# Gate rows, Q squares, row writes and the first one-hot of a two-layer decoder trunk, reordered

## The reference, cut to what matters

```
h = concat(meta, x)                                   # (272, 1024)
# layer 0: mLSTM mixer, 4 heads, q/k width 128, v width 256
q, k, v, o, gates = split(rmsnorm(h) @ w_in)
gates = 15 * tanh((gates + b) / 15);  i, f = gates
b = cumsum(log_sigmoid(f));  the weight of key s for query t in a head:
    exp(b_t - b_s + i_s - m_t)  for s <= t,  m_t = running maximum
out = (sum of s(q,k) * weight * v) / max(|sum|, exp(-m_t)), rmsnorm, * sigmoid(o)
h += out @ w_out
h += moe(rmsnorm(h))
# layer 1: forgetting attention, 16 heads of 64, queries are the 256 real tokens
k, v, f_pre = split(rmsnorm(h) @ kv_w);  F = cumsum(log_sigmoid(f_pre + b_f))
p = softmax(rmsnorm(q) . rmsnorm(k) + F_t - F_s, causal)
h += (p @ v) @ w_o
h += moe(rmsnorm(h))
# moe: 4 groups of 4 experts; best group, the 2 best experts in it;
#      y = sum over both of gate * down(silu(x @ w_gate) * (x @ w_up)), expert width 256
```

## Time and profile before

| | |
|---|---|
| median of 3 runs | 614.47 us (613.95 to 614.58) |
| the profiled execution, in all | 614.16 us |
| its span, first to last instruction | 612.4 us |
| PE busy | 592.6 us, 97% of the span |
| DVE, ACT, POOL busy | 214.0, 146.7, 42.2 us |
| read from HBM | 146.27 MB, 244 GB/s over the span |
| mean granted clock of TensorE | 0.997 |

### The profile page before, as it was taken

One profiled execution on the slowest core, in us unless ns is written; L12 is line 12 of the kernel. 1 busy time (PEld: TensorE's weight loads), 2 busy tenths in 40 slices (PEclk: granted clock), 3 DMA queues, 4 the chain that ended last, 5 costly groups with the idle time before them and its releaser, 6 DMA issues.

```text
span 612.4 us, 8078 instructions
## 1 busy us (share of the span) xinstructions
PE 592.6 (97%) x3098; PEld 369.8 (60%) x3098; DVE 214.0 (35%) x621; ACT 146.7 (24%) x408; POOL 42.2 (7%) x87
## 2 busy tenths in 40 slices
PE   8998999999999999999998999999999899999996
PEld 4686878887764544444466777777777633333331
DVE  3343013331065444444364333333411443222222
ACT  3312123331141111111063333333411421111110
POOL 7010000000011100000003100000000111000000
PEclk9998999999999999999999999999999999999999
DMA  9979430034645999999998614030317599999971
GB/s 284 341 187 347 173 137 1 0 138 155 250 150 220 413 409 424 418 421 380 352 349 252 216 38 170 20 118 1 137 70 274 188 341 355 414 421 420 423 323 70
DMA packets 59123, 150.04 MB, mean 245 GB/s; under 512 B 10092, under 2 KB 42924, under 8 KB 46796
## 3 DMA queue, kind: packets, MB, share of 16 engines
q1 hardware_dynamic: 54384, 136.58, 60.0%
q0 software_dynamic: 2912, 10.64, 5.0%
q10 hardware_dynamic: 1788, 2.29, 1.1%
HBM read 146.27 MB, written 3.23 MB: 244 GB/s over the span
## 4 chain that ended last, share of the span: by engine, by line
PE 91%; DMA 3%; DVE 2%; ACT 2%; issue 1%; SPq 0%; DVEq 0%; ACTq 0%; POOLq 0%
PE bank L1384 38%; PE bank L1656 19%; PE bank L1684 9%; PE bank L1698 5%; PE bank L1628 3%; PE bank L1703 3%; PE bank L1488 1%; DMA qk_area<-xs,idx 1%; PE bank L1825 1%; DMA ring<-in_m_w_in 1%; PE bank L1838 1%; PE bank L1869 1%; PE bank L1865 1%; PE bank L1663 1%; PE bank L1525 1%
## 5 line engine op out<-in xcount | busy, mean ns | idle before, releaser
L1384 PE MATMUL bank<-hxT,ring 128*128 128x272 f32 x576 | 139.5, 397 | 1.2 <-ACT big L647 1.1
L1384 PEld LDWEIGHTS bank<-hxT,ring 128*128 128x128 f32 x576 | 109.0, 192 | 23.8 <-ACT big L647 1.5
L1656 PE MATMUL bank<-ring,gate_area 128*64 128x512 f32 x496 | 115.1, 597 | 0.0
L1656 PEld LDWEIGHTS bank<-ring,gate_area 128*64 128x64 f32 x496 | 34.5, 137 | 63.4 <-issue 62.6
L1384 PE MATMUL bank<-tok,ring 128*128 128x272 f32 (+1 forms) x256 | 59.6, 389 | 0.7 <-DVE tok L1361 0.6
L1684 PE MATMUL bank<-ring,gate_area 128*32 128x512 f32 (+1 forms) x368 | 58.0, 594 | 0.0
L1384 PEld LDWEIGHTS bank<-tok,ring 128*128 128x128 f32 x256 | 47.8, 190 | 11.8 <-issue 3.9
L1096 DVE TENSOR_TENSOR qk_area<-qk_area,bank 128x256 f32<-128x256 f32 x16 | 6.7, 421 | 92.3 <-ACT qk_area L750 92.3
L1684 PEld LDWEIGHTS bank<-ring,gate_area 128*32 128x32 f32 (+1 forms) x368 | 16.5, 119 | 36.3 <-issue 36.3
L533 POOL DMA_INDIRECT qk_area<-xs,idx x16 | 15.8, 985 | 316.4 <-DMA xs<-tok 204.2
L750 ACT ACTIVATE qk_area<-bank 128x256 f32<-128x256 f32 x16 | 6.2, 384 | 121.6 <-PE bank L1656 121.6
(11 more groups left out here) (301 smaller groups left out, 642.8 us busy)
## 6 DMA issues: line engine op xcount, KB each, us to landing
ring<-in_moe_w_gate SPq DMA_DIRECT2D x31, 1024.0 KB, 8.4
ring<-in_moe_w_up SPq DMA_DIRECT2D x31, 1024.0 KB, 11.5
ring<-in_moe_w_down SPq DMA_DIRECT2D x31, 1024.0 KB, 15.0
ring<-in_m_w_in SPq DMA_DIRECT2D x12, 1024.0 KB, 11.6
ring<-in_kv_w SPq DMA_DIRECT2D x8, 1024.0 KB, 12.0
ring<-in_m_w_out SPq DMA_DIRECT2D x4, 1024.0 KB, 13.2
ring<-in_f_w_q SPq DMA_DIRECT2D x4, 1024.0 KB, 12.0
ring<-in_f_w_o SPq DMA_DIRECT2D x4, 1024.0 KB, 7.3
```

Source lines behind the costliest of these rows:

```text
L1384: ins = pe.matmul(bank[c % 2][:, 0:n], w[:, k, half * P:half * P + P], x[:, k, 0:n], start=(k == 0), stop=(k == KB - 1))
L1656: ins = pe.matmul(bank[1][s, :], xgT[b % 2][:, q, s], unit_gate_up(us[par][0], q), start=(q == 0), stop=(q == KB - 1))
```

## The change

It has these parts:

- PE spreads the gate rows of heads 0 and 1 ahead of V's block 0 and those of heads 2 and 3 ahead of block 1. The odd heads' m rows go to bank 4 instead of bank 2, so head 1 waits for DVE's copy of `c_tok` (new semaphore `c_read`). The wait for the last read of an m row moves from V to the first scores.
- In layer 1's first turn ACT squares Q before it handles the forget gates.
- ACT no longer issues the writes of the rows. It signals `rows_made` after each tile and goes on; SP issues the writes, behind the loads of the first two pairs.
- PE folds the logits after half of the first tile's transposes.
- LIVE is added to the base of the places. The one-hot matrix of the first pair is made from the places of its two experts and `eall`, ahead of limits and choices, and only in the first choice's part of `sel`; its indices sum three products (layer 0) instead of six.
- The evacuation of the first half of the first pair's transposed rows is split in two.
- The three units beside the ring share one semaphore.

```diff
         def arrived(s):
             if s in BESIDE:
-                return sem(f"beside_arrived{BESIDE.index(s)}"), 16
+                return sem("beside_arrived"), 16 * len(BESIDE)
...
                 for b in (0, 1):
                     down(b)
+                tiles, n, off = tiles_of(l)
+                for t, rows, c0 in tiles:
+                    sp.wait_ge(*in_layer("rows_made", l, t + 1))
+                    r0 = (META, META + P, 0)[t] - off
+                    sp.dma_start(xs[l][r0:r0 + rows, :], tok[0:rows, t, :]).then_inc(sem("xs_written"), 16)
...
-                act.activation(emB[:, hd, :], bank[(7, 2)[hd % 2]][:, 0:NT], ACT.Exp, scale=2.0) \
+                act.activation(emB[:, hd, :], bank[(7, 4)[hd % 2]][:, 0:NT], ACT.Exp, scale=2.0) \
...
-                    link(ins)
-                    r0 = (META, META + P, 0)[t] - off
-                    act.dma_start(xs[l][r0:r0 + rows, :], tok[0:rows, t, :]).then_inc(sem("xs_written"), 16)
+                    ins.then_inc(sem("rows_made"), 1)
...
+                act.wait_ge(*in_layer("rows_made", l, len(tiles)))
                 act.sem_inc(sem("xr_read"), 1)
...
                     head_rstd(0, "kT", j, NT)
+                    head_square(1, "qT", j, SEQ)
                     if j == 0:
                         act.wait_ge(sem("gate_rows_dve"), 3)
                         link(act.activation(f_a, f_a, ACT.Exp, scale=-1.0))
                         act.activation(f_a, f_a, ACT.Ln, bias=1.0).then_inc(sem("gate_rows_act"), 1)
-                    head_square(1, "qT", j, SEQ)
...
-            link(ins)
+            ins.then_inc(sem("c_read"), 1)
+            dve.wait_ge(sem("c_read"), 1)
...
+                share = [P, nt, 2, CAP]
+                first = sel[:, 0, 0:nt, 0:P].rearrange("p t (e s) -> p t e s", e=2)
+                link(dve.tensor_tensor(first, iota_f[:, 0:P].rearrange("p (e s) -> p e s", e=2).unsqueeze(1).to_broadcast(share),
+                                       raw[:, :, 0:2].unsqueeze(3).to_broadcast(share), ALU.is_equal))
+                dve.tensor_tensor(first, first, eall[:, 0:nt, 0:2].unsqueeze(3).to_broadcast(share), ALU.mult) \
+                    .then_inc(sem("sel_ready"), 1)
                 lim = lim16[:, :].unsqueeze(1).to_broadcast(bc16) if l == 0 else lim16t[:, :, :]
                 link(dve.tensor_tensor(mk[:, 0:nt, :], raw, lim, ALU.is_lt))
-                link(dve.scalar_tensor_tensor(slots[:, 0:nt, :], mk[:, 0:nt, :], LIVE, raw, ALU.mult, ALU.add))
+                link(dve.tensor_tensor(slots[:, 0:nt, :], mk[:, 0:nt, :], raw, ALU.mult))
...
+                row_of_slot(l, 0, 0, 1, 1)
                 link(dve.tensor_reduce(tok4[:, 0:2, 0:nt], t16[:, :, 0:nt, :], AX.X, ALU.add))
-                ones = [P, 2, nt, P]
-                dve.tensor_tensor(sel[:, :, 0:nt, 0:P], iota_f[:, 0:P].unsqueeze(1).unsqueeze(1).to_broadcast(ones),
-                                  tok4[:, 0:2, 0:nt].unsqueeze(3).to_broadcast(ones), ALU.is_equal) \
-                    .then_inc(sem("sel_ready"), 1)
...
-                row_of_slot(l, 0, 0, 1, 1)
...
+                    w = 2 if b == 0 else 4
+                    for q in range(0, 4, w):
+                        dve.tensor_tensor(xgT[b % 2][:, q:q + w, :], bank[0][:, q * P:(q + w) * P].rearrange("p (q s) -> p q s", q=w),
+                                          gains_x[:, l, q:q + w].unsqueeze(2).to_broadcast([P, w, P]), ALU.mult) \
+                            .then_inc(sem("xT_read0"), 1)
...
-            for hd in range(MH):
+            def spread_gates(hd):
+                if hd == 1:
+                    pe.wait_ge(sem("c_read"), 1)
                 if hd >= 2:
                     pe.wait_ge(sem("warg"), hd - 1)
                     pe.wait_ge(sem("em_ready"), hd - 1)
...
-            pe.wait_ge(sem("em_ready"), MH)
             pe.wait_ge(sem("hT_in"), KB)
             for j in range(9):
+                if j < 2:
+                    spread_gates(2 * j)
+                    spread_gates(2 * j + 1)
                 if j < 8:
                     project("v0", j, xT, NT)
...
                     pe.wait_ge(sem("warg"), MH)
+                    pe.wait_ge(sem("em_ready"), MH)
...
-                stream_rows(*tiles[0])
+                stream_rows(*tiles[0], k1=KB // 2)
                 pe.wait_ge(*in_layer("lgT_ready", l, 1))
...
                 ins.then_inc(sem("lg_tr"), 1)
+                stream_rows(*tiles[0], k0=KB // 2)
...
-                    terms = [(c, t, rows) for c in (0, 1) for t, rows, _ in tiles]
+                    terms = [(c, t, rows) for c in ((0,) if part == 1 else (0, 1)) for t, rows, _ in tiles]
...
                         if b == 0 and q == 2:
+                            pe.wait_ge(*in_layer("xT_read0", l, 2))
                             rows_of_slots(3, 3, (2, 3))
```

More of the change, by code:

```diff
@@ L1075, in x_evac @@
                         dve.wait_ge(*in_layer("gu_done", l, b - 1))
-                    dve.tensor_tensor(xgT[b % 2][:, 0:4, :], bank[0][:, :].rearrange("p (q s) -> p q s", q=4),
-                                      gains_x[:, l, 0:4].unsqueeze(2).to_broadcast([P, 4, P]), ALU.mult) \
-                        .then_inc(sem("xT_read0"), 1)
+                    w = 2 if b == 0 else 4
[3 more added lines that the diff above has]
+                            .then_inc(sem("xT_read0"), 1)
                 def combine_weights(b):
@@ L1454, in _ @@
                     .then_inc(sem("negM_mm"), 1)
-                pe.matmul(bank[(7, 2)[hd % 2]][:, 0:NT], negsel2[:, hd, :], row_m, start=True, stop=True) \
+                pe.matmul(bank[(7, 4)[hd % 2]][:, 0:NT], negsel2[:, hd, :], row_m, start=True, stop=True) \
                     .then_inc(sem("em_mm"), 1)
-            pe.wait_ge(sem("em_ready"), MH)
             pe.wait_ge(sem("hT_in"), KB)
             for j in range(9):
+                if j < 2:
+                    spread_gates(2 * j)
+                    spread_gates(2 * j + 1)
                 if j < 8:
@@ L1534, in moe, with stream_rows @@
                 per = 8 if l == 0 else 4
-                def stream_rows(t, rows, c0):
-                    for k in range(KB):
+                def stream_rows(t, rows, c0, k0=0, k1=KB):
+                    for k in range(k0, k1):
                         ins = pe.transpose(bank[(4, 6, 0)[t] + k // 4][0:rows, (k % 4) * P:(k % 4 + 1) * P],
@@ L1623, in rows_to_cols @@
                         if b >= 1:
-                            pe.wait_ge(*in_layer("xT_read0", l, b + 1))
+                            pe.wait_ge(*in_layer("xT_read0", l, b + 2))
                         else:
@@ L1631, in gate_up @@
                 def gate_up(b):
-                    pe.wait_ge(*in_layer("xT_read0", l, b + 1))
+                    pe.wait_ge(*in_layer("xT_read0", l, b + 2 if b else 1))
                     if b >= 1:
```

12 lines of the change are left out of this document (6 added, 6 removed).

## The result

The changed kernel takes 609.4 us (median of 5 runs, 608.07 to 610.52), against 614.58 (613.95 to 620.45, 5 runs) of the kernel before on the same chip: a ratio of 0.9891, 95% interval 0.9855 to 0.9927. The profiled execution took 609.40 us with a span of 607.5, 4.76 less than the 614.16 of before. The forecast was 607.9 with a range of 606.5 to 610.2: the direction and the largest terms were right, the sum 1.5 us too large. The result lies in the wide range, but outside the 607.1 to 608.9 that the forecast itself was given, and next to the 609.6 of rivals A and B; A did not happen, and B did only in one of the two layers.

The account below looks back on a forecast made before the run. PE, 91% of the chain, was taken to bound the kernel, which ends earlier only where PE idles, runs at half clock or does less. Gains 2.7 + 1.7 + 0.85 + 0.2 + 0.75 = 6.2 from 614.16 gave 607.9 us, range 606.5 to 610.2.

Parts of the forecast that it names:

- Rival A: The clock falls all the same, at V or at another place: 609.6 us, chance 0.13.
- rival B: Routing gains don't come: the closer writes land no earlier, or DVE's new order holds PE; 609.6 us, chance 0.12.
- Parts 1 and 2: Layer 0's gate rows and V: spreading them between V's blocks gains 2.7 us, and the full clock behind it 1.7.
- Part 3: Layer 0's routing: earlier fold, writes by SP and the new one-hot let the gather leave earlier, gain 0.85 us.
- Part 4: Layer 1's start: squares of Q ahead of the forget gates bring V 1.0 us earlier, but only 0.2 is gained.
- Rival E: Layer 1's start: the forget sums are no limit and the Q squares give their whole 1.0; 607.1 us, chance 0.07.
- Part 5: Layer 1's routing: the writes bind alone; earlier fold, one gap of 0.44 and the split evacuation gain 0.75 us.
- Rival C: End of each layer's output projection: the writes stand behind weights on SP's queue, the slower side; 619.8 us, chance 0.03.

Follow-up runs that it names:

- ACT's writes: The changed kernel with the three row writes issued by ACT again, each after its own completion: 609.3 us, ratio 0.9872.
- old matrix: The changed kernel with the first pair's old one-hot matrix (both choices, after the limits, six products): 613.57 us in one run, total not used because PE stalled.
- late fold: The changed kernel with all eight transposes of the first tile ahead of the fold of the logits again: 607.93 us in one run.
- without the Q squares: The changed kernel with ACT squaring Q behind the forget gates again, as before: 610.39 us, ratio 0.9885.
- pool kernel: The changed kernel with GpSimd masking the third pair's forget sums only after DVE scaled the first pair's probabilities: 608.97 us, and 608.88 when profiled again.

## Why the prediction was mostly right, and where it failed

**Parts 1 and 2 (4.4, measured 4.05).** Clock 1.7: measured 1.69. Order 2.7: measured 2.36. The bound of 2.3 had the cause, a cost for each switch to narrow matmuls, and I took the other value without a row for it. Rival A (the clock falls all the same) did not occur: in the changed kernel the windows fall below 1.00 only from 603 on, when PE's last product is over (601.7).

**Part 3 (0.85, measured 0.67).** The step that failed: "The later of them is the third write", and the one-hot "has no gain of its own here". Before, both limits stood at the same place; after, the index was the later one. The third write's issue is 2.22 ahead of the gather (173.29 and 175.51), as ACT's third is in the kernel with ACT's writes (168.97 and 171.17), and the index is 1.04 ahead, as in all kernels where it binds. Each edit alone is worth 0 to 0.24 (old matrix 9.28, ACT's writes 9.01, before 9.25), both together 0.71 of the gather, which is what the matrix moves the index (8.21 to 7.50). The writes did what the forecast said of them: the third landed 1.11 earlier (8.93 to 7.82, forecast 1.15); the gather could not use it. The operations' 0.56 was right, and PE and DVE were not late behind the gather. The 0.1 for the split evacuation was nothing: from the gathered rows on PE to gate/up it takes 1.46 before and 1.45 after. That 0.67 came near 0.85 is in part luck: the forecast took some 0.4 off its 1.15 for a lateness behind the gather that did not come.

**Part 4 (+0.2, measured -0.38, below the bound of -0.3).** "V starts 1.0 earlier": 0.85. "Next is late" the forget sums' DMA: right, it releases the first score in the row above, and the score came 0.08 earlier, where 0.25 was forecast. What the prediction left out is DVE behind it. It took the time from the first score to the transposes as fixed, but there DVE meets POOL's masks. Its scalings started 0.07 earlier and took 0.45 longer (1.69 before, 2.14 after): that is the -0.38. The masks started 0.40 later than before, counted from K, and this did more for the overlap than DVE's 0.07; that the edit itself moved them is not shown, as the late fold has the edit and masks at 24.40. So what the edit is worth hangs on that landing: -0.38 in the changed kernel, 0.58 in the late fold, 0.88 against before with the masks out of the way. Rival E's price (1.0) was near what could be had, but not its reason: the forget sums do hold the first score. There was slack behind it: without the Q squares the scalings end 0.56 ahead of the transposes, which follow PE's own projection.

**Part 5 (0.75, measured 0.35).** "The writes bind alone" was right: index and one-hot don't matter there. The mis-sized terms are the gap of 0.44, worth 0 by the kernel with ACT's writes, and the 0.1 of the split evacuation, worth 0 here too (1.46 before and after). That is rival B in one layer: the writes, closer together, land no earlier there (7.86 and 7.83), as one of 16 closing packets is late in both, while in layer 0 the third lands 0.89 earlier (8.71 and 7.82).

**Rival C** did not occur; SP's first write goes out when the first tile is made. Behind the kernel's first load of weights (a wait of 0.6 us) no stage shows PE waiting for a transfer of weights.

The errors, 0.35 + 0.18 + 0.58 + 0.40 = 1.51 too much, are the distance from 607.9 to 609.4. The rest is small: the tail was 0.2 shorter, and 0.14 of the span's gain is not in the whole time (4.9 and 4.76).

## What to carry to other kernels

Where an instruction waits for two chains, take the distance from each chain's end to it in more than one place before naming the one that binds; two edits, one on each chain, were worth 0 and 0.24 us alone and 0.71 together. When an edit moves VectorE's work, look what GpSimd does in its new place: a job that a DMA's landing releases can fall beside it and double VectorE's time, its moment can differ by a microsecond between profiles, and one wait on GpSimd makes sure of the order. When a DMA's issue is moved forward, look at its landing: 1.14 us of earlier issue gave 0.89 in one layer, and 0.52 gave 0.03 in the other.

## What the runs showed of the hardware that I had not expected

- VectorE's scaling of 128x272 took 0.37 us with GpSimd idle and up to 0.93 with GpSimd's masks beside it.
- PE can stand still inside a projection for want of instructions: 1.73 and 2.42 us in 2 of 14 profiles, both in K's first projection of layer 1. A transfer of 0.02 MB on the queue "instruction" starts between 301.2 and 302.8 in nine of the shifted kernels; in these two it started at 306.7 and 307.6, with DMA full at 343 to 358 GB/s. It took 1.09 us in all of them, and PE resumed 1.5 and 1.4 us after its end. The pool kernel's second profile, same program, had it at 302.4 and no stall. That the late packet is the cause is inferred from this order of events, no run forced it. The Trainium skill, "Runtime: NRT & Kernel Launch", section "Instruction fetch mechanics", states that an engine's instructions are refilled in blocks of 16 KiB by a DMA queue, mostly hidden; the size agrees, and here it was not always hidden.
- The last closing packet of a 512 KB write came 0.3 to 0.7 us behind the other fifteen (7.40 against 7.11, 7.38 against 6.72, above), and the gather waits for it.
- The narrow matmuls' switch cost of about 0.2 us each way, and layer 0's first gather's 1.04 us from the start of its index, where the second one needs 0.43 (172.84 to 173.27 in the changed kernel).
